# Two transformer blocks with expert routing: gelu stores through SP's queue, routing one half of the tokens at a time, gates cleared in the latent attention

## The reference

```python
def peer(h, w_q, sub_keys, expert_u, expert_v):
    q = (xt @ w_q).reshape(T, PEER_HEADS, 2, PEER_DQ // 2)
    s = jnp.einsum('thpd,hpnd->thpn', q, sub_keys)
    s_half, i_half = lax.top_k(s, PEER_TOPK)
    cand = s_half[:, :, 0, :, None] + s_half[:, :, 1, None, :]
    cand_idx = i_half[:, :, 0, :, None] * PEER_NKEYS + i_half[:, :, 1, None, :]
    top_s, pos = lax.top_k(cand, PEER_TOPK)
    idx = jnp.take_along_axis(cand_idx, pos, axis=-1)
    g = jax.nn.softmax(top_s, axis=-1)
    a = jnp.einsum('cd,ced->ce', xc, expert_u[idx])
    w = g * jax.nn.gelu(a)
    return jnp.einsum('ce,ced->cd', w, expert_v[idx])
```

## Time and profile before

| | us |
|---|---|
| median of 3 runs | 3717.65 (3714.27 to 3719.58) |
| the profiled execution, its own time | 3711.69 |
| its span in the trace | 3709.9 |
| PE busy | 3319.0 (89%) |
| ACT busy | 1471.7 (40%) |
| DVE busy | 2029.6 (55%) |
| POOL busy | 547.1 (15%) |

### The profile page before, as it was taken

How to read it: one execution, slowest core, us unless ns; L and a number is a source line. 1 busy time by engine, 2 the same in 40 slices (tenths; PEclk the granted TensorE clock), 3 DMA queues, 4 the chain that set the end, 5 groups by cost and what they waited for, 6 DMA issues and landing times.

```text
span 3709.9 us, 50142 instructions
## 1 busy us (share of the span) xinstructions
PE 3319.0 (89%) x21070; PEld 3024.1 (82%) x21070; DVE 2029.6 (55%) x2847; ACT 1471.7 (40%) x1851; POOL 547.1 (15%) x364
## 2 busy tenths in 40 slices
PE   5978999997353569999999999999999899999998
PEld 4767899997353569988888887898999799999996
DVE  5766548883121134566666666555446555555556
ACT  3335444443111134444444444444444454444443
POOL 2100000078888720000000000000000000000000
PEclk8989999998776789999999999999999999999999
DMA  8313555676454466676666655544455555555554
GB/s 321 119 46 101 164 190 190 203 199 149 69 103 67 105 215 207 211 248 243 238 238 234 237 190 176 182 154 162 148 181 181 193 168 190 188 188 187 187 189 153
DMA packets 214961, 659.43 MB, mean 178 GB/s; under 512 B 56096, under 2 KB 56096, under 8 KB 212176
## 3 DMA queue, kind: packets, MB, share of 16 engines
q1 hardware_dynamic: 160928, 581.96, 47.9%
q0 software_dynamic: 53808, 74.27, 8.3%
HBM read 620.35 MB, written 35.78 MB: 177 GB/s over the span
## 4 chain that ended last, share of the span: by engine, by line
PE 67%; POOL 12%; issue 3%; DVE 3%; ACT 1%; DMA 1%; DVEq 0%; ACTq 0%; POOLq 0%
PE bank L1284 67%; POOL scr_g L2205 12%; DVE wlo L1705 1%; DMA scr_g<-M 1%; PE bank L1326 1%; ACT whi L1474 1%; ACT M L1464 0%; DMA M<-scr_g 0%; POOL scr_a L2214 0%; DVE TMP L1768 0%; DVE R L2133 0%; DVE TMP L1769 0%; ACT M L1516 0%; DVE AL L1745 0%; DVE ST L1783 0%
## 5 line engine op out<-in xcount | busy, mean ns | idle before, releaser
L1705 DVE TENSOR_TENSOR wlo<-raw,whi 128x1024 fp32r<-128x1024 f32 x1101 | 1349.2, 1229 | 1375.5 <-ACT whi L1474 1371.9
L1474 ACT ACTIVATE whi<-raw 128x1024 fp32r<-128x1024 f32 x1101 | 1159.5, 1059 | 1404.8 <-PE bank L1284 1399.0
L1284 PE MATMUL bank<-AH,whi 128*128 128x256 f32 (+1 forms) x4112 | 1181.7, 287 | 253.2 <-DVE wlo L1705 252.8
L1284 PE MATMUL bank<-AL,whi 128*128 128x256 f32 (+1 forms) x4112 | 1171.4, 285 | 0.0
L1284 PE MATMUL bank<-AH,wlo 128*128 128x256 f32 (+1 forms) x4112 | 1171.2, 285 | 0.0
L1284 PEld LDWEIGHTS bank<-AH,whi 128*128 128x128 f32 (+1 forms) x4112 | 797.1, 194 | 258.3 <-DVE wlo L1705 255.2
L1284 PEld LDWEIGHTS bank<-AL,whi 128*128 128x128 f32 (+1 forms) x4112 | 797.2, 194 | 0.9
L1284 PEld LDWEIGHTS bank<-AH,wlo 128*128 128x128 f32 (+1 forms) x4112 | 796.4, 194 | 0.1
L1284 PE MATMUL bank<-whi,BH 128*128 128x512 f32 (+1 forms) x1608 | 625.7, 389 | 0.5 <-DVE wlo L1705 0.4
L1284 PE MATMUL bank<-wlo,BH 128*128 128x512 f32 (+1 forms) x1608 | 623.6, 388 | 0.0
L1284 PE MATMUL bank<-whi,BL 128*128 128x512 f32 (+1 forms) x1608 | 623.3, 388 | 0.0
(11 more groups left out here) (238 smaller groups left out, 1953.6 us busy)
## 6 DMA issues: line engine op xcount, KB each, us to landing
raw<-in_peer_u SPq DMA_DIRECT2D x256, 512.0 KB, 4.2
raw<-in_peer_v SPq DMA_DIRECT2D x256, 512.0 KB, 3.6
raw<-in_w_in SPq DMA_DIRECT2D x160, 512.0 KB, 3.3
raw<-in_w_up SPq DMA_DIRECT2D x128, 512.0 KB, 3.9
raw<-in_w_down SPq DMA_DIRECT2D x128, 512.0 KB, 3.4
raw<-in_w_out SPq DMA_DIRECT2D x64, 512.0 KB, 4.1
raw<-in_w_in_a SPq DMA_DIRECT2D x32, 512.0 KB, 5.7
scr_g<-M POOLq DMA_DIRECT2D x8, 2048.0 KB, 35.4
```

The costliest lines, as they stand in the source:

```text
L1284: return e.matmul(outp, l, r, start=start, stop=stop)
L1474: e.activation(whi[:, n % NH, :], raw[:, n % NR, :], ACT.Copy).then_inc(s_hi, 1)
L1705: e.tensor_tensor(wlo[:, n % NH, :], raw[:, n % NR, :], bf(whi[:, n % NH, :]), ALU.subtract).then_inc(s_lo, 1)
```

## The change

1. `gate_blank` and the eight `gate_clear` are emitted in the latent attention's stage, not at the start.
2. The gelu store is issued by SP, and two steps of `yield` later in the written order (in the third step of the next unit).
3. Half 0 is routed completely before half 1 begins (`i16_cast` for each half), so that its ids come in step 40 and those of half 1 in step 80.
4. One scatter task emits four scatters in each step, and changes the half after each round where both halves are routed and the other one has rounds left.

```diff
@@ after norm_T of x @@
-            go("gate_blank")
-            t_blank = up("POOL", "gate_blank")
-            for c in range(8):
-                go("gate_clear", c, fresh("POOL", t_blank))
-                t_clear = landing("gate_cleared")
@@ latent attention @@
             om_free = everyone()
+            go("gate_blank")
+            t_blank = up("POOL", "gate_blank")
+            for c in range(8):
+                go("gate_clear", c, fresh("POOL", t_blank))
+                t_clear = landing("gate_cleared")
@@ scatter @@
-            def scatter(t, ready):
-                landed = t_clear
-                for h in range(8):
-                    for k in range(16 * h, 16 * h + 16):
-                        go("gate_scatter", t, k, fresh("POOL", ready, landed if k % 16 == 0 else None))
+            routed = []
+
+            def scatter():
+                landed, rounds, t = [t_clear, t_clear], [0, 0], 1
+                while len(g_written) < 2:
+                    while not routed:
+                        yield
+                    if len(routed) == 2 and rounds[1 - t] < 8:
+                        t = 1 - t
+                    elif len(routed) == 1:
+                        t = 0
+                        if rounds[0] == 8:
+                            yield
+                            continue
+                    h = rounds[t]
+                    for k in range(16):
+                        go("gate_scatter", t, 16 * h + k, fresh("POOL", routed[t], landed[t] if k == 0 else None))
                         mark = landing(f"gate_scattered{t}")
-                        if k % 2:
+                        if k % 4 == 3:
                             yield
-                    landed = mark
-                g_written.append(landed)
+                    landed[t] = mark
+                    rounds[t] += 1
+                    if rounds[t] == 8:
+                        g_written.append(mark)
@@ routing @@
             def routing():
+                tasks.append(scatter())
                 for t in range(2):
                     for hp in range(16):
                         go("top16", SC[:, t, hp, :], V16[:, t, hp, :], I16u[:, t, hp, :], fresh("DVE", t_sc, everything))
                         last = up("DVE", "top16")
                         yield
-                go("i16_cast", fresh("DVE", last))
-                last = up("DVE", "i16_cast")
-                for t in range(2):
+                    go("i16_cast", t, fresh("DVE", last))
+                    last = up("DVE", "i16_cast")
                     for h in range(8):
...
-                    tasks.append(scatter(t, [tg, up("DVE", "expert_ids")]))
+                    routed.append([tg, up("DVE", "expert_ids")])
                     yield
@@ u_post @@
                 accs.give(pair, tg)
-                go("gelu_store", j, gi, fresh("POOL", tg))
-                a_written[j] = landing(f"gelu_stored{gi}")
-                gel_slots.give(gi, a_written[j])
+
+                def later():
+                    yield
+                    yield
+                    go("gelu_store", j, gi, fresh("SP", tg))
+                    a_written[j] = landing(f"gelu_stored{gi}")
+                    gel_slots.give(gi, a_written[j])
+                tasks.append(later())
@@ the function gelu_store moves unchanged from the POOL program to the SP program @@
```

More of the change, by code:

```diff
@@ L1954, in top16, with i16_cast @@
                 e.max_index(outi[:, 8:16], outv[:, 8:16], vals).then_inc(sem("top16"), 1)
-            def i16_cast(ready):
+            def i16_cast(t, ready):
                 for mark in ready:
                     e.wait_ge(*mark)
-                e.tensor_copy(I16, I16u).then_inc(sem("i16_cast"), 1)
+                e.tensor_copy(I16[:, t], I16u[:, t]).then_inc(sem("i16_cast"), 1)
             def candidates(t, h, ready):
@@ L2208, in gate_scatter @@
                                      ).then_inc(sem(f"gate_scattered{t}"), 16)
[L2210 to L2215, removed]
             def fetch(sc, ready):
@@ L2242, in gpsimd_program @@
                   "gate_blank": gate_blank, "gate_clear": gate_clear, "gate_scatter": gate_scatter,
-                  "gelu_store": gelu_store, "fetch": fetch, "load_lam": load_lam,
+                  "fetch": fetch, "load_lam": load_lam,
                   "na_bias": na_bias, "load_post": load_post})
@@ L2257, in load_piece, with gelu_store @@
                 e.dma_start(raw[:, m % NR, :], D[name][k, :, :]).then_inc(s_raw[m % NR], 16)
+            def gelu_store(j, gi, ready):
+                for mark in ready:
+                    e.wait_ge(*mark)
+                h = j % 2
+                e.dma_start(D["scr_a"][j // 2, :, 1024 * h:1024 * h + 1024],
+                            gels[gi].rearrange("p k n -> p (k n)")).then_inc(sem(f"gelu_stored{gi}"), 16)
             def store(j, t, ready):
@@ L2267, in end @@
                     e.wait_ge(*mark)
-            walk({"load_inputs": load_inputs, "load_piece": load_piece, "store": store, "end": end})
+            walk({"load_inputs": load_inputs, "load_piece": load_piece, "gelu_store": gelu_store, "store": store, "end": end})
         walk({})
```

## The result

The changed kernel takes 3758.74 us in the median (3753.21 to 3759.44, four runs) against 3716.55 for the kernel before: a ratio of 1.011 with a 95% interval of 1.0092 to 1.0127. It is **slower by 42 us**, which is clear of the spread but small (1.1%); the forecast was 21 us slower. The profiled execution took 3759.18 us, its span is 3757.4.

The account below looks back on a forecast made before the run. POOL's gate scatters were taken to set the time from 880 to 1330 us, though PE's products hold 67% of the span. 3711.7 + 40 (stretch) - 19 (clears) = 3733 us, 3738 against the median; range 3693 to 3792.

Parts of the forecast that it names:

- The store's wait: ACT's gelu waiting for gelu stores queued behind POOL's scatters: 239.1 us in 8 waits, to vanish completely.
- The stretch: Expert units beside POOL's scatters, to the last gelu store: one PE stop of about 310 us, +40 us in sum.
- POOL's end: End of POOL's 16 scatter rounds: 6.3 before DVE stops, 9.7 at 31.3 us after, done at 1248.8 us.
- the four terms: Scatter rounds POOL does while DVE still works: 1.5, 0.9, 1.1 and 2.7, given as 6.3.
- the "estimate" for the rounds beside half 1's `top16`: Scatter rounds during 52.7 us of half 1's `top16` steps, at the mean of 31.3 and 38.0 us: 1.5 rounds.
- PE's 113 pieces: PE's work left in the stretch after its stop: 1 + 14 x 8 pieces, 329.8 us.
- The clears: Gate clears leaving the kernel's start: 5 us, 11.5 us and about 2 us, together -19, between -12 and -22.
- The 2 us that I gave for the low clock: At the start, PE's restart at the low clock goes with the distance wait: about 2 us saved, estimated.
- DVE does not slow the scatters: Faster rival: scatters keep their pace beside a working DVE; stretch -16, total -35, 3683 us; chance 0.18.
- Landing stays slow: Slower rival: landing waits of 4.83 us persist and all rounds beside DVE are slow; +82, 3800 us; chance 0.15.
- SP is held by the stores: Rival: stores hold SP, so piece loads come late; matters only above 11.5 us at a time; chance 0.03.
- the lost 272.7 us: Stalls and slow clock between the stores of units 8 and 22: 595.3 us taken, 322.6 needed; the most any cure gives.

Follow-up runs that it names:

- e1: The kernel before with only the gelu store moved from POOL to SP: 3704.6 us, ratio 0.9967.
- e5: The changed kernel with the gelu store given back to POOL: 3747.1 us, ratio 1.0082 to the kernel before.
- e2: The kernel before with only the gate clears moved to the latent attention: 3703.9 us, ratio 0.9961.
- e8: e4 with DVE forming only 64 of 1024 low-part columns for nearly all expert_u pieces, the rest left out of the products: 3427.4 us.
- e6: e4 with half 0 stopped after 3 rounds until half 1 is routed, so the halves alternate: 3505.4 us, ratio 0.9433 to the kernel before.
- e4: The changed kernel with the first gate product emitted in the last step of unit 31: 3526.4 us, ratio 0.9489 to the kernel before.
- e3: The changed kernel with the first gate product emitted 32 steps later, at step 149: 3676.1 us, ratio 0.9891 to the kernel before.
- e7: The changed kernel with two scatters a step instead of four: 3602.3 us, ratio 0.9691 to the kernel before.
- e9: e4 with the gelu store given back to POOL: 3720.8 us, ratio 1.0005 to the kernel before.

## Why the prediction was right, and where it was off

**The direction and the mechanism** hold at each step. The halves never alternated: half 1's scatters stand strictly behind half 0's, and there are 14 landing waits. I wrote 15; the first round of half 1 has no round of its own half before it. DVE stopped after its split at 932.4 (forecast: 945 less the start's gain) and PE was released by it at 1264.57. The store's wait vanished and gave next to nothing for its 239.1 us: 12.4 us in e1, and in the changed kernel 11.7 us the other way (e5). SP held no load back. The reload found POOL free.

**The stretch was forecast at +40 and measured +55.6.** The failing term is POOL's end: 1248.8 in the clock of the kernel before, measured 1252.5 + 13.1 = 1265.6. Half 0's ids were no part of it: they were ready at 679.2 + 13.1 = 692.3 there, forecast 692.2, and the first scatter began 0.8 us later. By DVE's stop six rounds were done, not 6.3 (the four terms add up to 6.2). The term that was too large is the "estimate" for the rounds beside half 1's `top16`, for which the trace had no scatters: the first took 724.67 - 679.99 = 44.7 us, with a landing wait of 6.55, not 34.6. 0.3 of a round is 9 us. The ten rounds after it took 1252.5 - 933.9 = 318.6 us instead of 313: there are single pauses of about 1.9 us in place of 0.30, as the one before 968.46, five of them in the stop, 7.9 us together. Among the 256 scatters of the kernel before there is none. The pace of 31.2 in a round without one was right. PE's 113 pieces after the restart were right too: 1593.2 - 1264.6 = 328.6 us.

**The clears were forecast at -19 and gave -13.1** (e2: -13.1, by its median). The constants came 15.94 - 11.61 = 4.3 us earlier, not 5. The wait of 11.55 us went. But `distance` now runs on POOL (49.12 to 53.31) beside DVE's work instead of after it, and two DVE instructions that need 0.69 and 0.17 us took 1.75 and 1.74 at that time: 2.6 us back. By the first distance DVE is 72.94 - 59.98 = 12.96 us ahead, nearly all of the 13.1. The 2 us that I gave for the low clock were not there to win: from its restart to 110 us DVE waited for PE for only 1.1 us in the kernel before, so DVE and not PE set the pace.

**The total.** Both errors, 15.6 us in the stretch and 6 in the clears, went the same way, so the total came out 21 us over the forecast: the kernel is slower for the reasons given, by twice the 21 us named. One sentence of the forecast on its first rival is wrong: POOL's end at 1228 is where the whole kernel would break even with the start at -19. The stretch by itself gains only if POOL is done before 1551.6 - 329.8 - 13.1 = 1208.7.

**The rivals.** *DVE does not slow the scatters* is refuted by e8. The reading of the Trainium skill ("SBUF — State Buffer", section "Who interferes with whom"), that a tensor_tensor holds only the read side and so leaves descriptor generation alone, which the page itself calls inferred, does not hold for these indirect DMAs: 1553 against 2227 ns decides. The rule in the same section of the Trainium skill, that of two instructions that want the shared ports the one that has them blocks the other for its whole instruction, fits both directions seen here, DVE before POOL in the scatters and POOL before DVE at 49.81; the second was not tried apart. *Landing stays slow* did not come in the stop (waits of 1.68 to 1.89 us between rounds), only before it, with the loads and PE at work. *SP is held by the stores* did not come: the loads of a unit kept their 23 us.

**What the change could have had.** The forecast took the lost 272.7 us as the most that a cure could give, and called all of it out of reach for want of POOL's speed. As a bound it held: e6 is 211 us under the kernel before, some 13 of them from the clears. But "out of reach" was wrong, because it took the gate product's place as given. e4 and e6 take 232 and 253 us from the changed kernel by giving POOL more of PE's work to run beside; only the 21 us between them come from a quicker POOL.

## What to carry to other kernels

Where one written order feeds all engines, ask of every instruction that waits for a slow engine how much independent work stands behind it on its own engine. Removing the wait that a profile names is worth nothing if the next instruction waits for the same end (12 us of 239), and the same removal is worth 194 us once that instruction stands last. When a side task is made denser in the written order, what follows it comes earlier too, though the slow engine does not.

## What was not expected of the hardware

An indirect DMA's issue on POOL takes 1.55 us alone, and 2.2 us in the mean, up to 2.6, beside DVE splits of 1.2 us every 2.88 us (e4). So the slow engine ran at 31.2 us a round with its neighbours stopped and at about 46 with them at work. PE's stop was not all loss: without it (e4) POOL ended 94 us later and the kernel was 232 us faster, so the stop had paid back 94 of 326 us.

Single pauses of about 1.8 us and more, where the gap between two scatters is otherwise 0.30, stand in the changed kernel, e3, e4 and e8 before the same six of POOL's 256 scatters: the 61st, 114th, 121st, 189th, 242nd and 249th, whatever runs beside them. The last three are the first three 128 scatters on. In the changed kernel they are 1.79 to 1.93 us, five of them with DVE, PE and the loads standing; in e4 and e8, beside loads, up to 4.7 and 4.2. e7, with another order of the halves, has two, before the 61st and the 237th; e6, whose halves alternate, has one of 1.1 us. The kernel before, e2, e5 and e9, with gelu stores in POOL's stream, have none, and neither has e1, whose stores are on SP. So their places go by the order of what POOL issues and not by its neighbours' work; what makes them is not shown.
